# Row norms of a two-block model: parts summed ahead and fed as the root's bias, two norms in a row taken as one root, and five constant matmuls in place of eight

## What is computed

```python
EPS = 1e-6
def _rmsnorm(x, g):
    xf = x.astype(jnp.float32)
    y = xf * lax.rsqrt(jnp.mean(xf * xf, axis=-1, keepdims=True) + EPS)
    return (y * g.astype(jnp.float32)).astype(x.dtype)

# first block
for layer in range(2):
    x = x + layer_of(_rmsnorm(x, norm_g))          # even, then odd
x = _rmsnorm(x, final_norm)
# second block
h = rmsnorm(x, mix_norm)                           # a second norm right behind the first
x = x + mixer(h) @ w_mix_out
h = rmsnorm(x, xattn_norm); mem_n = rmsnorm(mem, mem_norm)
x = x + memory_xattn(h, mem_n, ...)
h = rmsnorm(x, ffn_norm)
x = x + conv_ffn(h, w_up, conv_w, w_down)
return rmsnorm(x, final_norm)
```

## Time and profile before

| | |
|---|---|
| Median of 3 runs | 2421.54 us (2421.45 to 2421.83) |
| The profiled execution, its own time | 2421.37 us |
| Its span in the profile | 2419.6 us |
| PE busy | 2388.1 us, 99% |
| PE weight loads | 2064.2 us, 85% |
| DVE busy | 1611.2 us, 67% |
| ACT busy | 1167.1 us, 48% |
| Granted TensorE clock, mean | 0.999 |

### The profile page before, as it was taken

The page is one execution under the profiler, slowest core; times in us unless marked ns, Lnnn a source line. Parts: engine busy times, 40 slices in busy tenths (PEclk is TensorE's granted clock), DMA queues, the critical chain, the costliest instruction groups (busy, mean ns, idle before and its releaser), DMA issues.

```text
span 2419.6 us, 35274 instructions
## 1 busy us (share of the span) xinstructions
PE 2388.1 (99%) x14027; PEld 2064.2 (85%) x14027; DVE 1611.2 (67%) x2030; ACT 1167.1 (48%) x1407; POOL 157.0 (6%) x142
## 2 busy tenths in 40 slices
PE   7999999999999999999999999999999999999998
PEld 6888988898888888889988888888888888888887
DVE  6999776555685876697655445455777467755764
ACT  6433674544565654642654344345554344433433
POOL 1000000000200100000000000000122002200220
PEclk9999999999999999999999999999999999999999
DMA  8565546454435555553175554444655555555554
GB/s 250 182 201 182 167 139 214 145 184 166 157 109 205 162 186 176 184 164 105 37 258 176 191 195 153 143 170 141 206 189 192 197 186 185 197 187 196 180 179 144
DMA packets 337333, 422.43 MB, mean 175 GB/s; under 512 B 8478, under 2 KB 263212, under 8 KB 336700
## 3 DMA queue, kind: packets, MB, share of 16 engines
q1 hardware_dynamic: 334204, 410.87, 51.2%
q0 software_dynamic: 2544, 8.52, 1.0%
q10 hardware_dynamic: 464, 1.32, 0.2%
HBM read 418.53 MB, written 2.10 MB: 174 GB/s over the span
## 4 chain that ended last, share of the span: by engine, by line
PE 97%; DVE 1%; ACT 1%; DMA 0%; issue 0%; POOL 0%; SPq 0%; ACTq 0%; DVEq 0%
PE ps L744 36%; PE ps L745 18%; PE ps L803 10%; PE ps L801 10%; PE ps L802 10%; PE ps L748 1%; PE ps L749 1%; PE ps L747 1%; PE ps L1096 1%; PE ps L1088 1%; PE ps L1309 1%; PE ps L1010 1%; PE ps L1300 1%; PE ps L1013 1%; DMA ring<-in_even_w_in 0%; PE ps L840 0%
## 5 line engine op out<-in xcount | busy, mean ns | idle before, releaser
L744 PE MATMUL ps<-h_cat,w_hi 128*128 128x512 f32 x3824 | 1342.5, 397 | 5.6 <-DVE h_cat L2283 4.8
L745 PE MATMUL ps<-h_cat,w_lo 128*128 128x256 f32 x3824 | 1062.8, 278 | 0.0
L744 PEld LDWEIGHTS ps<-h_cat,w_hi 128*128 128x128 f32 x3824 | 717.1, 188 | 176.9 <-issue 7.5
L745 PEld LDWEIGHTS ps<-h_cat,w_lo 128*128 128x128 f32 x3824 | 719.2, 188 | 2.2 <-issue 1.9
L2140 DVE TENSOR_TENSOR w_lo<-ring,w_hi 128x2048 fp32r<-128x2048 f32 (+2 forms) x279 | 588.5, 2112 | 177.4 <-ACT w_hi L1390 174.8
L1390 ACT ACTIVATE w_hi<-ring 128x2048 fp32r<-128x2048 f32 (+2 forms) x279 | 492.9, 1767 | 83.8 <-PE ps L803 63.2
L2136 DVE TENSOR_TENSOR w_lo<-ring,w_hi 128x2048 fp32r<-128x2048 f32 (+1 forms) x136 | 303.0, 2233 | 230.0 <-ACT w_hi L1387 227.2
L1387 ACT ACTIVATE w_hi<-ring 128x2048 fp32r<-128x2048 f32 (+1 forms) x136 | 252.4, 1862 | 271.3 <-PE ps L803 253.6
L801 PE MATMUL ps<-w_hi,h_cat 128*128 128x512 f32 x640 | 250.7, 392 | 0.0
L803 PE MATMUL ps<-w_hi,h_cat 128*128 128x512 f32 x640 | 249.3, 389 | 0.0
L802 PE MATMUL ps<-w_lo,h_cat 128*128 128x512 f32 x640 | 249.0, 389 | 0.0
(11 more groups left out here) (432 smaller groups left out, 2251.5 us busy)
## 6 DMA issues: line engine op xcount, KB each, us to landing
ring<-in_w_ffn_up SPq DMA_DIRECT2D x44, 2048.0 KB, 7.9
ring<-in_w_mix_in SPq DMA_DIRECT2D x28, 2048.0 KB, 8.0
ring<-in_even_w_in SPq DMA_DIRECT2D x27, 2048.0 KB, 7.9
ring<-in_w_ffn_down SPq DMA_DIRECT2D x16, 2048.0 KB, 8.0
ring<-in_odd_w_in SPq DMA_DIRECT2D x11, 2048.0 KB, 8.1
ring<-in_even_w_out SPq DMA_DIRECT2D x8, 2048.0 KB, 8.1
ring<-in_odd_w_out SPq DMA_DIRECT2D x8, 2048.0 KB, 8.0
ring<-in_w_mix_out SPq DMA_DIRECT2D x8, 2048.0 KB, 8.0
```

Source lines behind the costliest of these rows:

```text
L744: mm(o[:, 0:2 * T], whi[slot][:, k, :], flat(cat[:, k]), start=first, stop=False)
L745: ins = mm(o[:, T:2 * T], wlo[slot][:, k, :], cat[:, k, 0, :], start=False, stop=end)
```

## The change

The change touches all norms but the first one's sums. The squares are scaled by `D ** -0.5` before they are squared, so that parts are parts of the mean. For the halved norms and the final one, DVE adds the first three parts and eps to a new tile, `so_far`, as soon as the third group is squared, and the root is taken as `sqrt(part[3] + so_far)`, with `so_far` as the bias of the ACTIVATE; nothing of DVE stands between the last square and the root. For the two norms in a row, the product of both factors is written as one: with s1 and s2 as above, `1 / sqrt(s1 + eps) / sqrt(s2 / (s1 + eps) + eps)` is `1 / sqrt(s2 + eps * (s1 + eps))`. DVE forms `s2's three parts + eps * (s1 + eps)` as the bias while ACT squares x times gain. The first norm's own factor, which is needed later for x itself, is now made behind the norm: a root on ACT behind `halved_rows` and a reciprocal on DVE behind `turned_rows` (`inverse_first`). And PE has five matmuls of constants at norm 2 in place of eight.

```diff
@@ PE @@
-                for n in range({1: 4, 2: 8, 5: 4}[norm]):
+                for n in range({1: 4, 2: 5, 5: 4}[norm]):
@@ ACT @@
-            af(dump[:, st["squared"] % 2, :], tile, ACT.Square, accum_out=part[:, which, t, c:c + 1]).then_inc(sem["squared"], 1)
+            af(dump[:, st["squared"] % 2, :], tile, ACT.Square, scale=D ** -0.5, accum_out=part[:, which, t, c:c + 1]).then_inc(sem["squared"], 1)
...
-            af(root[:, which, :], root[:, which, :], ACT.Sqrt, bias=eps[:], scale=1.0 / D).then_inc(sem["std_ready"], 1)
+            af(root[:, which, :], root[:, which, :], ACT.Sqrt, bias=eps[:]).then_inc(sem["std_ready"], 1)
...
-        def root_of(t, totalled, count, std, which=0):
-
-            act.wait_ge(sem[totalled], count)
-            af(root[:, which, t:t + 1], root[:, which, t:t + 1], ACT.Sqrt, bias=eps[:], scale=1.0 / D).then_inc(sem[std], 1)
+        def root_of(t, based, std, which=0):
+
+            act.wait_ge(sem["squared"], st["squared"])
+            act.wait_ge(sem["based"], based)
+            af(root[:, 0, t:t + 1], part[:, which, t, 3:4], ACT.Sqrt, bias=so_far[:, which, t:t + 1]).then_inc(sem[std], 1)
...
-        root_of(1, "totalled", 3, "std_ready")
-        root_of(1, "totalled", 4, "std_ready", 1)
-        halved_rows(2, 4, S["o_out"], [row_of(x, c) for c in range(3)] + [last_row])
+        root_of(1, 4, "std_ready", 1)
+        halved_rows(2, 3, S["o_out"], [row_of(x, c) for c in range(3)] + [last_row])
+        act.wait_ge(sem["totalled"], 2)
+        af(root[:, 1, :], root[:, 1, :], ACT.Sqrt).then_inc(sem["std_ready"], 1)
@@ DVE @@
-        def total_of(t, squared, which=0):
+        def base(squared, which=0):
 
             dve.wait_ge(sem["squared"], squared)
-            return nc.vector.tensor_reduce(root[:, which, t:t + 1], part[:, which, t], AX_X, ALU.add)
+            ch.link(nc.vector.tensor_reduce(so_far[:, which, :], part[:, which, :, 0:3], AX_X, ALU.add))
+            return nc.vector.tensor_scalar(so_far[:, which, :], so_far[:, which, :], EPS, None, ALU.add)
...
             post_to(S[then].n0)
+            base(SQUARES[k] - 2).then_inc(sem["based"], 1)
             add_row(g, 0)
-            total_of(0, SQUARES[k] - 1).then_inc(sem["half_totalled"], 1)
-            inverse_of(0, "half_std", halves, tok_rstd).then_inc(sem["half_rstd"], 1)
+            inverse_of(0, "half_std", halves).then_inc(sem["half_rstd"], 1)
...
-        def two_norms(t, squared, totalled, std, rstd, count):
-
-            one, root1 = tok_rstd1[:, t:t + 1], root[:, 1, t:t + 1]
-            total_of(t, squared).then_inc(sem[totalled], 1)
-            ch.link(total_of(t, squared, 1))
-            inverse_of(t, std, count, tok_rstd1).then_inc(sem[rstd], 1)
-            dve.wait_ge(sem[rstd], count)
-            ch.link(tt(root1, root1, one, ALU.mult))
-            tt(root1, root1, one, ALU.mult).then_inc(sem[totalled], 1)
-            ch.link(inverse_of(t, std, count + 1, tok_rstd, 1))
-            tt(tok_rstd[:, t:t + 1], tok_rstd[:, t:t + 1], one, ALU.mult).then_inc(sem[rstd], 1)
-            dve.wait_ge(sem[rstd], count + 1)
+        def two_norms(t, squared, std, rstd, count):
+
+            dve.wait_ge(sem["squared"], squared)
+            first = root[:, 1, t:t + 1]
+            ch.link(tt(first, part[:, 0, t, 3:4], so_far[:, 0, t:t + 1], ALU.add))
+            stt(so_far[:, 1, t:t + 1], first, EPS, so_far[:, 1, t:t + 1], ALU.mult, ALU.add).then_inc(sem["based"], 1)
+            inverse_of(t, std, count).then_inc(sem[rstd], 1)
+            dve.wait_ge(sem[rstd], count)
...
+        def inverse_first():
+
+            dve.wait_ge(sem["std_ready"], 4)
+            nc.vector.reciprocal(tok_rstd1[:], root[:, 1, :]).then_inc(sem["rstd_ready"], 1)
+            dve.wait_ge(sem["rstd_ready"], 4)
...
         turned_rows(2, x)
+        inverse_first()
         seg("g_qkv", links=12)
```

More of the change, by code:

```diff
@@ L261, in build @@
     root = place("root", [P, 2, TT])
+    so_far = place("so_far", [P, 2, TT])
     tok_rstd = place("tok_rstd", [P, TT])
@@ L396, in build @@
              "row_ready", "emptied", "squared", "gained", "totalled", "std_ready", "rstd_ready", "scaled_dve", "scaled_act", "turned",
-             "scaled_one", "half_totalled", "half_std", "half_rstd", "ht_hi", "ht_ready", "tiles_read", "agate_read", "hhi_ready", "h_ready", "x_normed", "gain1_loaded", "gain_out_loaded",
+             "scaled_one", "based", "half_std", "half_rstd", "ht_hi", "ht_ready", "tiles_read", "agate_read", "hhi_ready", "h_ready", "x_normed", "gain1_loaded", "gain_out_loaded",
              "conv_tap", "bg_ready", "conv_total", "conv_mean", "conv_centred", "conv_sq", "conv_var", "conv_std", "conv_normed", "conv_silu",
@@ L1582, in halved_rows, with halved_norm @@
                     hi(k, 2 * c - 2), hi(k, 2 * c - 1)
-        def halved_norm(k, roots, halves, g, then):
+        def halved_norm(k, roots, based, g, then):
             drain_to(S[then].n0)
@@ L1588, in halved_norm @@
             square_row(g, 0)
-            root_of(0, "half_totalled", halves, "half_std")
+            root_of(0, based, "half_std")
             split_to(S[then].n0 + 3)
             square_row(g, 1)
-            root_of(1, "totalled", roots, "std_ready")
+            root_of(1, based, "std_ready")
             halved_rows(k, roots, g, [row_of(x, c) for c in range(4)])
@@ L2013, in _ @@
             if j == 7:
-                deviation(5, 1)
+                deviation(3, 1)
             if j == 8:
@@ L2023, in _ @@
         squares(g, 3)
-        deviation(6)
+        deviation(4)
         seg("x_k")
@@ L2077, in _ @@
         wide_seg("x_out", lambda c: squares(S["x_out"], c))
[L2078 removed]
+        halved_norm(5, 7, 5, S["x_out"], "f_up0")
         for p in range(3):
@@ L2308, in add_row, with inverse_of @@
             tt(v, v, pair(g, 3)[t][:], ALU.add).then_inc(sem["emptied"], 1)
-        def total_of(t, squared, which=0):
+        def base(squared, which=0):
             dve.wait_ge(sem["squared"], squared)
-            return nc.vector.tensor_reduce(root[:, which, t:t + 1], part[:, which, t], AX_X, ALU.add)
-        def inverse_of(t, std, count, rstd, which=0):
+            ch.link(nc.vector.tensor_reduce(so_far[:, which, :], part[:, which, :, 0:3], AX_X, ALU.add))
+            return nc.vector.tensor_scalar(so_far[:, which, :], so_far[:, which, :], EPS, None, ALU.add)
+        def inverse_of(t, std, count):
             dve.wait_ge(sem[std], count)
-            return nc.vector.reciprocal(rstd[:, t:t + 1], root[:, which, t:t + 1])
+            return nc.vector.reciprocal(tok_rstd[:, t:t + 1], root[:, 0, t:t + 1])
         def one_scaled(k, source):
@@ L2335, in halved_norm @@
             add_row(g, 1)
-            total_of(1, SQUARES[k]).then_inc(sem["totalled"], 1)
-            inverse_of(1, "std_ready", roots, tok_rstd).then_inc(sem["rstd_ready"], 1)
+            inverse_of(1, "std_ready", roots).then_inc(sem["rstd_ready"], 1)
             dve.wait_ge(sem["rstd_ready"], roots)
@@ L2635, in _ @@
         post_to(S["g_qkv"].n0)
-        def two_norms(t, squared, totalled, std, rstd, count):
-            one, root1 = tok_rstd1[:, t:t + 1], root[:, 1, t:t + 1]
-            total_of(t, squared).then_inc(sem[totalled], 1)
-            ch.link(total_of(t, squared, 1))
-            inverse_of(t, std, count, tok_rstd1).then_inc(sem[rstd], 1)
-            dve.wait_ge(sem[rstd], count)
-            ch.link(tt(root1, root1, one, ALU.mult))
-            tt(root1, root1, one, ALU.mult).then_inc(sem[totalled], 1)
-            ch.link(inverse_of(t, std, count + 1, tok_rstd, 1))
-            tt(tok_rstd[:, t:t + 1], tok_rstd[:, t:t + 1], one, ALU.mult).then_inc(sem[rstd], 1)
-            dve.wait_ge(sem[rstd], count + 1)
+        def two_norms(t, squared, std, rstd, count):
[4 more added lines that the diff above has]
+            inverse_of(t, std, count).then_inc(sem[rstd], 1)
+            dve.wait_ge(sem[rstd], count)
         last = x[:, 1, 3 * WIDE:]
+        ch.link(base(SQUARES[2] - 4))
+        dve.wait_ge(sem["squared"], SQUARES[2] - 4)
+        ch.link(nc.vector.tensor_reduce(so_far[:, 1, :], part[:, 1, :, 0:3], AX_X, ALU.add))
+        dve.sem_inc(sem["based"], 1)
         add_row(S["o_out"], 0)
@@ L2964, in _ @@
         down = S["f_down2"]
+        base(SQUARES[6] - 2).then_inc(sem["based"], 1)
         add_row(down, 0)
-        total_of(0, SQUARES[6] - 1).then_inc(sem["half_totalled"], 1)
-        inverse_of(0, "half_std", 5, tok_rstd).then_inc(sem["half_rstd"], 1)
-        dve.wait_ge(sem["half_rstd"], 5)
+        inverse_of(0, "half_std", 4).then_inc(sem["half_rstd"], 1)
+        dve.wait_ge(sem["half_rstd"], 4)
         gained_scaled(0, slice(0, 3 * WIDE))
```

17 lines of the change are left out of this document (8 added, 9 removed).

## The result

The changed kernel takes 2427.3 us (median of 12 runs, 2426.6 to 2430.7) against 2421.7 us of the kernel before on the same chip (12 runs, 2421.3 to 2422.7): ratio 1.0027, 95% interval 1.0019 to 1.0035. The prediction said 2419.9 us, 0.07% faster, in a range of 2419.2 to 2420.9; by the medians the kernel became 5.6 us slower, and the interval of the ratio doesn't reach 1. (A ratio, with its interval, is formed from all the executions, and need not be that of the medians.) The twelve runs lie in two groups, seven from 2426.6 to 2427.5 and five from 2430.0 to 2430.7, with the same granted clock of 0.999.

The account below looks back on a forecast made before the run. PE, busy for 99% of the span, was taken as the bound, so only its waits at norms and the end count: 1.31 + 3 x 0.12 = 1.67 us, 2421.54 - 1.67 = 2419.9 us, range 2419.2 to 2420.9.

Parts of the forecast that it names:

- the sum: Whole kernel: 1.31 + 3 x 0.12 = 1.67 us saved, with PE the bound again and no norm's gain lost behind it.
- What it adds: Extra DVE instructions ahead of each norm, ACT root and DVE reciprocal behind norm 2: covered by waits or slack, costed at nothing.
- the clock: Rival: behind norm 2, fewer constants drop PE's granted clock to 1.2 GHz, adding 6.8 us, 2426.6 us; chance 0.02.
- Norm 2's gain: At norm 2, one root and one reciprocal remain, so tile 1's transposes start 1.31 us earlier; bounds 1.19 and 1.37.
- The idle time ahead of the transposes: Sign at norm 2: PE idles near 0.33 us before tile 1's transposes; much more or zero would refute the prediction.
- the ten rows of constants: Sign at norm 2: PE's five constant matmuls, ten rows in the timeline, take about 2.3 us.
- the second instruction of the bias: Sign at norm 2: the second of DVE's two small instructions forming the bias ends 0.4 us ahead of the root.
- the 1.42 us behind: PE's second idle time at norm 2, behind the transposes while ACT and DVE copy turned tiles; said to move as a whole.
- the own wait: Norms 1, 5 and final: ACT's root waits for ACT's own square, 0.28 us from read to root, saving 0.12 each.
- Own wait as a full handover: Rival: ACT's root starts 0.03 us behind the read's end; each place saves 0.18, norm 2 1.37; 2419.6 us, chance 0.10.
- The five constants: At norm 2: five constant matmuls earn nothing by themselves; with eight only 0.35 of the 1.31 us would come through.
- What was costed at nothing: Added DVE instructions ahead of norms, and root and reciprocal behind norm 2, where over 4 us of slack stand against 0.3.

Follow-up runs that it names:

- the kernel without the move: Changed kernel with `so_far` put into free bytes so no other tile moves: 2418.98 us against 2421.06 for the kernel before (0.9991); on another chip 2420.07 against 2421.91 (0.9993).

## Why the prediction was wrong

**The step that failed** is the sum, which lacks a term for the placing of `so_far`. "What it adds" priced only the instructions that the change issues, and "The sum" took "From here on PE is the bound again, and what is gained in a norm is not lost behind it" as its end; what the new tile does to the place of the tiles behind it, and so to PE's matmuls, was put at nothing without a reason. Measured, that term is +7.9 us of matmuls by the profile (6.6 to 7.4 by the times), and 3.3 us more in some executions; against it stands a gain of 1.95 us. No rival ended there: the one on the slower side was the clock, which stayed at its full level in the windows of norm 2 in the profile after.

**Norm 2's gain** was right: forecast 1.31, measured 1.36 between the rows and 1.37 at the next matmuls. The idle time ahead of the transposes is 0.27 where I had 0.33, the ten rows of constants take 2.32 as forecast (2.3), the second instruction of the bias ends at 796.02, 0.37 ahead of the root (0.4), and the 1.42 us behind are unchanged. What was off is ACT's wait for its own square (the own wait).

**The own wait** costs less than I took from norm 0. Read to root is 0.21 to 0.22 us, not 0.28, so norms 1, 5 and the end give 0.19, 0.20 and 0.19 in place of 0.12, and the four places give 1.95 us, not 1.67. The rival "Own wait as a full handover" had 1.91 and was right; I gave it 0.10. The Trainium skill, Perfetto Trace Analysis, section on the per-engine timelines (DVE / Act Engine Instruction), says that the update of a semaphore is globally propagated and visible to all engines, which makes no exception for the engine's own wait; the trace agrees: 0.21 and 0.22 us from the read to ACT's own root here, and 461.45 - 461.24 = 0.21 from the read to DVE's reduction before. Why the root of norm 0 starts 0.28 behind its read the earlier trace rows stays open: it waits for two semaphores, as the new roots do. The lesson is that one row from another place was taken against many rows of handovers.

**The five constants** behave as said: with eight, 0.86 us of the gain is held back (0.96 by the working), with three nothing is added. That the cut "earns nothing by itself" is right as well (1.0002); in the one profiled execution with the old chain the clock fell behind it, but the runs don't show that the cut did that.

**What was costed at nothing** costs nothing in the end: in the kernel without the move the matmuls are 1.3 us early behind norm 2 and 1.5 us ahead of norm 5, so the added root, the reciprocal and the bases are covered. (Between, up to 0.4 us is lost and regained in the narrow segments from 1467 to 1600 us; that and the 0.2 us in small steps I did not follow up.)

**What stays open.** Why the offset matters inside the chip isn't shown by these runs, only that it does. Nor is it shown why the narrow pairs of the first stage lose 3.3 us in some executions of the kernels that are moved by 32 or 64 bytes (9 of 19 runs of the changed kernel), though their own two operands keep their distance; nor why, with the weights moved by 32, some narrow segments lose and others don't. The traces do say what a narrow pair costs: from the start of one to the start of the next, 347 ns where it is fast and 353 ns where it is slow, the same 6.6 ns as for a wide matmul. In the kernel before, with all distances at multiples of 256, the first stage runs at 347, but the segment at 960 us at 350, a mixture. With `h_cat` 32 bytes further from the weights both run at 347, and its gain of 4.6 us comes from such mixed segments; with the weights moved towards `h_cat` by 32 both run at 353. So a multiple of 256 isn't the best distance for the narrow pairs here, and what the sign of the offset does was tried with no other value. For the wide matmuls the tried distances give one picture, for the narrow pairs there is no rule.

## What to carry to other kernels

A diff's `place` or allocation line is an edit like any other: ask which tiles it moves, and whether PE is the bound while it reads them; here 32 bytes cost four times what the rest of the change earned. When a change makes PE busier without more instructions, group matmuls by form before looking for waits: a few nanoseconds on a thousand instructions show there and nowhere in the waits. Put small new tiles into free bytes, or pad until the distances differ from the old ones by a multiple of 256 bytes; the changed kernel is then 1.5 to 2.1 us faster than the kernel before in three comparisons, less than 0.1%. Two of the three intervals reach past 1 and the third ends at it; the traces show the gain place by place.

## What the hardware showed that I had not expected

A matmul of 128x512 fp32r elements behind another costs 5.6 to 6.6 ns more (389 to 395 or 396 ns by the profile; 0.233 against 0.227 us from start to start) when the distance from its stationary to its moving operand, a multiple of 256 bytes in a partition before, is changed by 32, 64 or 128 bytes. Changed by 256 or 512 it costs nothing, and moving both operands costs nothing; other remainders weren't tried. That holds for the wide matmuls, whose stationary operand is a tile of activations, and as said not for all the narrow ones. The Trainium skill, TensorE: Matmul & The Clock Gate, Part 2, says that the two operands have read ports of their own, and that loading the next weights takes no read bandwidth from the running matmul. The runs don't bear that out for every placement: how long the matmul takes depends on where its two operands lie to each other, also with nothing else at work. What in the chip does it, they don't show.
